# HGRN2 in a hybrid mixer kernel: chunks of 64 tokens, half-block scaling and one predicated copy

## The reference, cut to what matters

```python
def _hgrn2(q, k, v, logf, S0):
    L = _chunk_len(q.shape[1])                 # 64 for the prompt, 4 for the samples
    def step(S, inp):
        qc, kc, vc, fc = inp
        g = jnp.cumsum(fc, axis=2)
        dec = _masked_exp(g[:, :, :, None, :] - g[:, :, None, :, :], incl)
        a = jnp.einsum('bhlc,bhmc,bhlmc->bhlm', qc, kc, dec)
        o = (jnp.einsum('bhlc,bhcv->bhlv', qc * jnp.exp(g), S)
             + jnp.einsum('bhlm,bhmv->bhlv', a, vc))
        gl = g[:, :, -1:, :]
        S = S * jnp.exp(gl[:, :, 0, :, None]) + jnp.einsum('bhlc,bhlv->bhcv', kc * jnp.exp(gl - g), vc)
        return S, o
```

## Time and profile before

| what | value |
|---|---|
| median of 3 runs (lowest, highest) | 1358.6 us (1355.88, 1361.22) |
| profiled execution | 1358.13 us, span 1356.2 us, mean TensorE clock 0.945 |
| PE busy | 1245.6 us, 92% of the span |
| DVE busy | 611.0 us, 45% |
| ACT busy | 377.3 us, 28% |
| DMA | 117.13 MB, mean 86 GB/s |

### The profile page before, as it was taken

One profiled execution on the slowest core, in us unless ns is written; L12 is line 12 of the kernel. 1 busy time (PEld: TensorE's weight loads), 2 busy tenths in 40 slices (PEclk: granted clock), 3 DMA queues, 4 the chain that ended last, 5 costly groups with the idle time before them and its releaser, 6 DMA issues. The chain is left out here.

```text
span 1356.2 us, 24614 instructions
## 1 busy us (share of the span) xinstructions
PE 1245.6 (92%) x10509; PEld 1108.0 (82%) x10509; DVE 611.0 (45%) x1249; ACT 377.3 (28%) x563; POOL 11.6 (1%) x30
## 2 busy tenths in 40 slices
PE   5599989989999996688999999987999999989997
PEld 2478767767777783478999999887999999989996
DVE  1352754566577877445323334445222222353233
ACT  1431451452122221245222222114223223341112
POOL 0001100000000000000000000000000000000000
PEclk9799989989999995588999999998999999989999
DMA  9713422213321301057333323131322333123301
GB/s 306 243 34 93 99 94 95 94 39 122 122 92 31 98 2 32 1 101 136 106 99 85 78 90 97 33 86 40 94 73 81 93 93 83 57 71 87 86 22 66
DMA packets 191025, 117.13 MB, mean 86 GB/s; under 512 B 36650, under 2 KB 189351, under 8 KB 190550
## 3 DMA queue, kind: packets, MB, share of 16 engines
q1 hardware_dynamic: 190358, 115.68, 30.4%
q0 software_dynamic: 576, 0.14, 0.1%
HBM read 108.84 MB, written 6.96 MB: 85 GB/s over the span
## 5 line engine op out<-in xcount | busy, mean ns | idle before, releaser
L746 PE MATMUL ps<-scr_parts 128*128 128x272 f32 x2688 | 522.5, 293 | 18.8 <-DVE hT_parts L2321 8.9
L746 PEld LDWEIGHTS ps<-scr_parts 128*128 128x128 f32 x2688 | 429.6, 191 | 24.4 <-issue 13.3
L746 PE MATMUL ps<-hT_parts,scr_parts 128*128 128x272 f32 x1408 | 391.3, 291 | 0.0
L2223 DVE TENSOR_TENSOR scr_parts<-ring,scr_parts 128x1024 fp32r<-128x1024 f32 (+1 forms) x100 | 128.9, 1289 | 309.1 <-ACT scr_parts L1512 305.8
L746 PEld LDWEIGHTS ps<-hT_parts,scr_parts 128*128 128x128 f32 x1408 | 262.0, 190 | 0.0
L1512 ACT ACTIVATE scr_parts<-ring 128x1024 fp32r<-128x1024 f32 (+1 forms) x100 | 111.1, 1111 | 501.8 <-PE ps L746 492.1
L746 PE MATMUL ps<-hT,ring 128*128 128x272 f32 x960 | 243.3, 407 | 3.0 <-ACT pj L1381 3.0
L746 PEld LDWEIGHTS ps<-hT,ring 128*128 128x128 f32 x960 | 182.0, 195 | 43.4 <-ACT pj L1381 3.1
L746 PE MATMUL ps<-pj_parts,scr_parts 128*128 128x272 f32 x992 | 169.2, 295 | 5.7 <-DVEq L1639 5.7
L746 PEld LDWEIGHTS ps<-pj_parts,scr_parts 128*128 128x128 f32 x992 | 143.2, 192 | 7.3 <-DVEq L1639 6.3
L746 PE MATMUL ps<-scr 64*64 64x64 f32 (+10 forms) x1768 | 101.9, 260 | 21.4 <-DVEq L1639 17.9
(11 more groups left out here) (312 smaller groups left out, 1056.3 us busy)
## 6 DMA issues: line engine op xcount, KB each, us to landing
ring<-in_w_in_dram SPq DMA_DIRECT2D x62, 512.0 KB, 6.4
ring<-in_ada_w_dram SPq DMA_DIRECT2D x48, 512.0 KB, 6.7
ring<-in_ffn_w_in_dram SPq DMA_DIRECT2D x44, 512.0 KB, 4.6
ring<-in_ffn_w_out_dram SPq DMA_DIRECT2D x16, 384.0 KB, 3.3
ring<-in_ffn_w_out_dram SPq DMA_DIRECT2D x16, 320.0 KB, 3.9
ring<-in_w_out_dram SPq DMA_DIRECT2D x8, 512.0 KB, 4.7
x_scratch<-scr SPq DMA_DIRECT2D x1, 2176.0 KB, 13.4
Q<-x_scratch SPq DMA_DIRECT2D x1, 2176.0 KB, 11.2
```

Source lines behind the costliest of these rows:

```text
L746: return pe.matmul(out, lhsT, rhs, start=start, stop=stop, skip_group_check=True)
L2223: dve.tensor_tensor(lo, src, hi.bitcast(F32), SUB).then_inc(w_split, 1)
```

## The change

HGRN2 goes over the prompt in chunks of 64 tokens. A tile of 128 tokens stays the unit of work, but its two chunks lie side by side in the partitions (128 = 2 x 64 keys), the level of 64 goes away, and the state is handed from one chunk to the next inside the tile. Each level scales only the half blocks it needs (keys of first halves, queries of second halves) into one buffer hQK, takes the differences with the sign that makes Exp enough (no Abs), and writes its entries into hD by one predicated copy from PSUM with the level's mask of 64 columns; hX and the addition are gone. The 128-column masks leave the constants (2514 to 1618 columns). `gdn_levels` becomes `levels_of`, which is the same six levels for GDN. The planner's costs of the HGRN2 stages are changed.

```diff
-LEVELS = [1, 2, 4, 8, 16, 32, 64]
-GDN_LEVELS = 6
+LEVELS = [1, 2, 4, 8, 16, 32]
...
-K_M64, K_NEG64, K_ID64, K_N = 2002, 2386, 2450, 2514
+K_M64, K_NEG64, K_ID64, K_N = 1106, 1490, 1554, 1618
...
-    s += [("dec", "act"), ("kd", "dve"), ("tok", "pe"), ("tokc", "dve"), ("out", "pe"), ("outc", "dve")]
-    if t == NT:
-        s += [("state", "pe"), ("statec", "dve")]
+    s += [("dec", "act"), ("kd", "dve"), ("tok", "pe"), ("tokc", "dve")]
+    if t < NT:
+        s += [("out0", "pe"), ("outc0", "dve"), ("out1", "pe"), ("outc1", "dve")]
+    else:
+        s += [("out", "pe"), ("outc", "dve"), ("state", "pe"), ("statec", "dve")]
...
-... "h_diag": 1.0, "h_sc": 0.9, "h_add": 1.8, ... "h_qk": 0.75, "h_dec": 0.8, "h_tokc": 0.82, "h_out": 1.6, "h_outc": 1.8,
+... "h_diag": 1.0, "h_sc": 0.6, "h_add": 1.0, ... "h_qk": 0.5, "h_dec": 0.45, "h_tokc": 0.65, "h_out0": 0.9, "h_outc0": 0.5, "h_out1": 0.6, "h_outc1": 0.9,
...
+            def block_scores(t, bank, keys, queries):
+                l = DK if t < NT else NS
+                for p in range(2):
+                    for r in blocks_of(t):
+                        for q in range(2):
+                            last = mm(ps[r, bank + q, p * l:(p + 1) * l], keys[half(q), p, r], queries[half(q), p, r])
+                return last
+
+            def chunk_outputs(bank, vals, at, kd):
+                for p in range(2):
+                    for q in range(2):
+                        for b in range(2):
+                            h, r = 2 * p + q, half(b)
+                            mm(ps[half(q), bank + b, p * DK:(p + 1) * DK], vals[r, h * DK:(h + 1) * DK],
+                               at[r, (2 * q + p) * DK:(2 * q + p + 1) * DK], p == 0, False)
+                for p in range(2):
+                    for q in range(2):
+                        for b in range(2):
+                            h, r = 2 * p + q, half(b)
+                            last = mm(ps[half(q), bank + b, 256 + p * DK:256 + (p + 1) * DK], kd[r, h * DK:(h + 1) * DK],
+                                      vals[r, h * DK:(h + 1) * DK], False, False)
+                return last
+
+            def state_outputs(bank, states, qs):
+                for b in range(2):
+                    for p in range(2):
+                        for q in range(2):
+                            last = mm(ps[half(q), bank + b, p * DK:(p + 1) * DK], states[b][half(q), p, :], qs[half(q), p, half(b)],
+                                      False, p == 1)
+                return last
...
-                        act.activation(hEf[:, 0:2 * w], hEf[:, 0:2 * w], ACT.Abs)
-                        act.drain()
-                        act.activation(hEf[:, 0:2 * w], hEf[:, 0:2 * w], ACT.Exp, scale=-1.0).then_inc(hgrn_s, 1)
+                        act.activation(hEf[:, 0:2 * w], hEf[:, 0:2 * w], ACT.Exp).then_inc(hgrn_s, 1)
...
-                    for t in range(NT):
-                        c = slice(t * P, t * P + P)
-                        dve.tensor_tensor_scan(pj[:, HF + f, c], ones, a_[:, c], 0.0, MUL, ADD)
+                    for n in range(T // DK):
+                        c = slice(n * DK, (n + 1) * DK)
+                        dve.tensor_tensor_scan(pj[:, HF + f, c], ones[:, 0:DK], a_[:, c], 0.0, MUL, ADD)
...
+            def carry(S_next, S, e, b, bank):
+                for p in range(2):
+                    dve.scalar_tensor_tensor(out=S_next[:, p, :], in0=S[:, p, :], scalar=e[:, p, b:b + 1],
+                                             in1=ps[:, bank + b, 256 + p * DK:256 + (p + 1) * DK], op0=MUL, op1=ADD)
...
                     def level_diff(n):
                         s = LEVELS[n]
-                        for p in range(2):
-                            x = g[:, p, :].rearrange("k (b i) -> k b i", i=2 * s)
-                            dve.tensor_tensor(f(hEf)[:, p, :].rearrange("k (b i) -> k b i", i=2 * s), x,
-                                              x[:, :, s - 1:s].to_broadcast([P, w // (2 * s), 2 * s]), SUB)
+                        x, e = (b.rearrange("k p (b i) -> k p b i", i=2 * s) for b in (g, E_))
+                        mid = x[:, :, :, s - 1:s].to_broadcast([P, 2, w // (2 * s), s])
+                        dve.tensor_tensor(e[:, :, :, 0:s], mid, x[:, :, :, 0:s], SUB)
+                        dve.tensor_tensor(e[:, :, :, s:2 * s], x[:, :, :, s:2 * s], mid, SUB)
...
-                    for q in range(2):
-                        dve.tensor_tensor(D_[:, 2 * q:2 * q + 2, :], ps[0:w, 6 + q, 0:2 * w].rearrange("m (p l) -> m p l", p=2),
-                                          ident[0:w, 0:w].unsqueeze(1).to_broadcast([w, 2, w]), MUL)
+                    dve.tensor_tensor(heads(hD), score, every(in_block(K_ID64, t)), MUL)
...
-                        dve.tensor_tensor(f(hQl), pj[:, HQ:HQ + 2, c], f(hEf), MUL)
-                        dve.tensor_tensor(f(hKl), kg[:, :, c], f(hEf), MUL)
+                        dve.tensor_tensor(out[:, :, :, 0:s], pairs(kg[:, :, c])[:, :, :, 0:s], e[:, :, :, 0:s], MUL)
+                        dve.tensor_tensor(out[:, :, :, s:2 * s], pairs(pj[:, HQ:HQ + 2, c])[:, :, :, s:2 * s], e[:, :, :, s:2 * s], MUL)
...
-                        X_ = v(hX)
-                        for q in range(2):
-                            dve.tensor_tensor(X_[:, 2 * q:2 * q + 2, :], ps[0:w, 6 + q, 0:2 * w].rearrange("m (p l) -> m p l", p=2),
-                                              mask(n, w).unsqueeze(1).to_broadcast([w, 2, w]), MUL)
+                        dve.copy_predicated(heads(hD), every(in_block(K_M64 + n * DK, t).bitcast(U32)), score)
...
-                        dve.drain()
-                        dve.tensor_tensor(D_, D_, X_, ADD)
...
-                    dve.tensor_copy(hKd[0:w, 0:256], ps[0:w, 6, 0:256])
-                    dve.tensor_copy(hV[0:w, 0:256], ps[0:w, 6, 256:512])
+                    dve.tensor_copy(hKdV[0:w, :], ps[0:w, 6, :])
...
+                    if t < NT:
+                        for b, (S, S_next) in enumerate(((S_h, S_h1), (S_h1, S_h))):
+                            hgrn.begin(dve, t, f"h_outc{b}")
+                            carry(S_next, S, eH, b, 6)
+                            if b == 1:
+                                dve.tensor_copy(pj[:, HI:HI + 2, c].rearrange("k p (b l) -> k b p l", b=2),
+                                                ps[:, 6:8, 0:P].rearrange("k b (p l) -> k b p l", p=2))
```

More of the change, by code:

```diff
@@ L131, in gdn_stages @@
          ("lower", "dve"), ("first", "pe"), ("t1", "act")]
-    for n in gdn_levels(t)[1:]:
+    for n in levels_of(t)[1:]:
         s += [(f"x{n}", "pe"), (f"xc{n}", "act"), (f"y{n}", "pe"), (f"upd{n}", "dve")]
@@ L185, in levels_of @@
     return range(len(LEVELS)) if t < NT else range(2)
-def gdn_levels(t):
-    return range(GDN_LEVELS) if t < NT else range(2)
 def blocks_of(t):
@@ L226 @@
 COST = {"pe": 1.2, "dve": 1.2, "act": 0.9}
-COSTS = {"g_scale": 2.3, "g_diff": 0.9, "g_lower": 1.9, "g_upd": 1.2, "g_uc": 0.5, "h_diag": 1.0, "h_sc": 0.9,
-         "h_add": 1.8, "s_diff": 2.4, "s_att": 2.6, "s_conv": 3.6, "g_conv": 3.6, "s_ri": 16.0, "g_l2sq": 2.4, "g_l2m": 2.4,
+COSTS = {"g_scale": 2.3, "g_diff": 0.9, "g_lower": 1.9, "g_upd": 1.2, "g_uc": 0.5, "h_diag": 1.0, "h_sc": 0.6,
+         "h_add": 1.0, "s_diff": 2.4, "s_att": 2.6, "s_conv": 3.6, "g_conv": 3.6, "s_ri": 16.0, "g_l2sq": 2.4, "g_l2m": 2.4,
          "h_b": 2.2, "h_g": 3.0, "h_ls": 2.6, "h_ln": 2.6, "h_silu": 3.0, "s_rb": 3.0, "g_y": 0.95, "s_w": 8.0,
@@ L1052, in hgrn_pe @@
                     hgrn.begin(pe, t, "h_qk")
-                    scores(t, 6, kg[:, :, c], pj[:, HQ:HQ + 2, c]).then_inc(hgrn_s, 1)
+                    block_scores(t, 6, kg[:, :, c], pj[:, HQ:HQ + 2, c]).then_inc(hgrn_s, 1)
                     yield
@@ L1056, in hgrn_pe @@
                         hgrn.begin(pe, t, f"h_qk{n}")
-                        scores(t, 6, f(hKl), f(hQl)).then_inc(hgrn_s, 1)
+                        block_scores(t, 6, f(hQK), f(hQK)).then_inc(hgrn_s, 1)
                         yield
@@ L2056, in hgrn_dve @@
                     hgrn.begin(dve, t, "h_kd")
-                    dve.tensor_tensor(f(hEf), kg[:, :, c], f(hEf), MUL)
-                    keep_last(eH, f(hQ), t, w, 2)
+                    dve.tensor_tensor(E_, kg[:, :, c], E_, MUL)
+                    if t < NT:
+                        dve.tensor_copy(eH[:, :, 0:2], f(hQ)[:, :, DK - 1:P:DK])
+                    else:
+                        keep_last(eH, f(hQ), t, w, 2)
                     dve.drain()
```

90 lines of the change are left out of this document (45 added, 45 removed).

## The result

The changed kernel takes **1303.05 us** (median of 4 runs, 1301.98 to 1305.8) against 1359.8 (4 runs, 1355.88 to 1361.22): ratio 0.959, 95% interval 0.9563 to 0.9617. The profiled span is 1302.1 us, 54.1 shorter.

The account below looks back on a forecast made before the run. HGRN2's serial chain was taken to end the mixer, with a slow-clock tail from 510 to 581 us to shrink. Gates 35.9 us earlier plus 1.4 at the start, off 1358.1, gave 1321 us, range 1309 to 1348.

Parts of the forecast that it names:

- The copy at the multiplication's price: VectorE, each HGRN2 level: the predicated copy taken at 0.42 us, with bounds 0 and 1.75 us.
- the level's period: HGRN2's serial path: one level goes from 4.88 us to 3.09 us.
- VectorE's sum: VectorE from 298 to 581 us: 46 to 47 of 194 us of work saved, 24%.
- GDN's tile at 72 us: GDN's tiles from 353.0 us on shorten from 87 to 72 us each, since VectorE is less loaded.
- HGRN2 is still the last chain: Mixer's end: sign of being wrong; the forecast had HGRN2 done near 518 us, before GDN.
- the start's 1.4: Kernel start: 448 KB less of constants bring 1.4 us, bounds 0 and 2.1.
- TensorE: no gain but 0.03 ... Net TensorE 3 us less: HGRN2's TensorE stages: halved scores gain only 0.03 us a level; net 3 us less work, bounds 0 and 8.
- the packed floor: TensorE from 298 us: 231.5 us of work plus 3.8 idle, so the mixer ends no sooner than 533.
- both limits fall on 534 ... I add 6.: Mixer's end: GDN's end and packed TensorE both limit at 534 us; 6 us margin gives 540.
- Where GDN is last, h_hi stands before high(0): 7.4.: After the mixer: ScalarE's h_hi activations follow GDN, so the first gate matmul comes 7.4 us later, at 547.4.
- TensorE packed to the end: Rival: GDN done earlier, units fill TensorE, mixer ends near 534, total 1310 us; chance 0.12.
- the last rival: Planner order: chains speed up but units still go first, leaving a 70 us low-clock tail; 1347 us, within chance 0.20.

Follow-up runs that it names:

- before_dve2: Kernel before with one more 128x256 VectorE multiplication from PSUM per HGRN2 level, result unused: 1366.43 us, ratio 1.0063.
- after_dve2: Changed kernel with one more 128x256 VectorE multiplication from PSUM per HGRN2 level, result unused: 1303.06 us, ratio 0.9599 to the kernel before.
- form128: Changed kernel with six levels' scores again as 8 instructions of 64x128 and the predicated copy in two halves: 1314.37 us, ratio 0.9684 to the kernel before.
- before_newcosts: Kernel before, no instruction changed, with the planner's new costs for HGRN2's stages: 1355.66 us, ratio 0.9984.
- after_oldcosts: Changed kernel, same instructions, with all of the planner's old costs for HGRN2's stages: 1335.71 us, ratio 0.9829 to the kernel before.
- half128: Kernel before with predicated copy, signed half blocks in one buffer, no Abs and adjusted planner costs, still 128 tokens and seven levels: 1325.57 us, ratio 0.9765.

## Why the prediction was right in kind and too slow

**Right.** The copy at the multiplication's price (0.443 against 0.42); the level's period (2.9 against 3.09); VectorE's sum (45 us of the 46 to 47); GDN's tile at 72 us (331.7 to 404.1); the part after the mixer at 773 us; the clock at 0.98 to 510 us. That VectorE's part of HGRN2 stops being what the rest waits for is right in substance: before_dve2 shows a price for it before, after_dve2 none after.

**Named signs that failed.** HGRN2 is still the last chain, by 5.6 us, which the prediction names as a sign of being wrong. The units ended at 521.5 and not past 525, and the gates started at 528.9 and not at 543 to 555.

**Wrong, and by how much.** The gates were forecast at 547.4, and at 546.0 with the start's 1.4 taken off; they started at 528.9. The 18.5 us to 547.4 come from three terms:

- *"TensorE: no gain but 0.03 ... Net TensorE 3 us less"*, and from it the packed floor, "298 + 235 = 533. No order of the work ends the mixer sooner." This is the step that failed most. From 298 us to the end TensorE is busy 208.15 + 13.38 = 221.5 us, not 231.5. With the first window's idle 3.8 us that puts the floor at 523.3, 9.7 us lower. I priced HGRN2's stage of sixteen at 0.61 us by the earlier trace rows, and that row is GDN's, which uses two quarters of the array; HGRN2's uses four and takes 0.28 to 0.39. form128 gives 8.6 us for just this term, over the bound of 8 that I had set for all of TensorE. The output stage was priced by the same kind of row: 1.08 for 32 matmuls that use four quarters and take 0.62. The other part of the 9.7 is 2.7 us of work that TensorE has done before 298 us (253.59 us there against 250.90), which the 1.4 of the start stands for in part. The Trainium skill, TensorEngine Tiling (Array Packing), section Theoretical Speedup, would have had me save some 8 us more, and I set it aside for the row that spoke against it. The runs bear its size out: the 0.32 us that I estimated for a stage by it lies between the measured 0.28 and 0.39.
- *"both limits fall on 534 ... I add 6."* The mixer's last step ended at 525.96, 2.7 above the floor in place of 7 (540 less 533): 4.3 us. GDN was not the limit I made it. Its running tile ended at 331.7 and not at 343.5, since the new costs leave HGRN2 less work on paper, so that it no longer takes the first turns from GDN (351.4 with the old costs); its last tile took 59.7 and not 72. The samples took 56.6 and not 46. It was done at 520.3.
- *"Where GDN is last, h_hi stands before high(0): 7.4."* HGRN2 remained the last chain, by 5.6 us; h_hi was hidden behind it, and 2.9 us followed: 4.5 us.

9.7 + 4.3 + 4.5 = 18.5. The last two terms are the prediction's own margins between limits; the runs show their sizes, and not which single wait made them. The 7.4 itself is borne out where GDN does end last: 7.5 us in before_newcosts. The rival "TensorE packed to the end" had the right mechanism, with a floor 10 us too high; it had 0.12.

**Right for less than the whole reason.** I let the lists follow the work and gave the planner's costs no term: only the last rival names a planner that "still sends the units first and leaves a 70 us tail". after_oldcosts is that case: its last unit ends at 505.1, 59 us before the gates, and it costs 33 us. That the costs in this diff fit the new work is thus more than half of the gain, and nothing in my working priced that.

## What to carry to other kernels

Where an order is laid out from a table of costs, a faster stage is worth what the table knows of it: price the new costs as an edit of their own, and test instructions and costs separately before crediting either. Price a short TensorE stage by a row of a stage that lies in the array in the same way: the same form and count on other quarters was half as dear again, and the kernel before had a fitting row. Before adding margins to two limits, ask what the order will hide behind the later one.

## What the runs showed of the hardware that was not expected

- A predicated copy of 128x256 from PSUM by a mask repeated over four heads takes 0.443 us, no more than the multiplication (0.419), and 0.34 from start to start; in half128 one of 128x512 takes 0.73 (0.62 from start to start).
- Sixteen float32 matmuls of 64x64 that use all four quarters of the array take 0.39 us between stages of another form and 0.28 ahead of one of their own; sixteen that use two quarters take 0.61, and eight of 64x128 0.64. The order of the quarters makes 0.02 us.
- The lead from 448 KB less of constants at the start, 1.5 us at 13 us, was down to 0.8 us at 75 and stayed so to 183 us; from 183 to 192 us the execution with the larger constants was granted 0.62 in place of 0.81, and the difference grew by 1.5 us.
